# Embedding tiles, quarter tiles and early output chunks placed in TensorE's waits of a two-block transformer kernel

## The reference

```python
x = x + concat([rms(mla), rms(diff) * (1 - lam_init), rms(chunk)]) @ w_out[l]
x = x + conv_ffn(rms(x), ...)
# second block
x = layer_norm(ALPHA * x + h, ln1_g, ln1_b)
x = layer_norm(ALPHA * x + mlp(x) + sigmoid(x @ w_ple_gate + b) * (p[l] @ w_ple), ln2_g, ln2_b)
```

## Time and profile before

| what | value |
|---|---|
| median of 3 runs | 3014.87 us (3014.5 to 3016.16) |
| profiled execution | 3012.1 us, its span 3010.4 us |
| TensorE busy | 2929.3 us, 97% |
| VectorE, ScalarE, POOL busy | 1367.7, 840.3, 1363.9 us |
| mean granted clock of TensorE | 0.989 of full |
| chain that ended last | TensorE 93%, VectorE 3%, ScalarE 2% |

### The profile page before, as it was taken

The page is one execution under the profiler, slowest core; times in us unless marked ns, Lnnn a source line. Parts: engine busy times, 40 slices in busy tenths (PEclk is TensorE's granted clock), DMA queues, the critical chain, the costliest instruction groups (busy, mean ns, idle before and its releaser), DMA issues.

```text
span 3010.4 us, 40838 instructions
## 1 busy us (share of the span) xinstructions
PE 2929.3 (97%) x14072; PEld 2409.9 (80%) x14072; DVE 1367.7 (45%) x3149; ACT 840.3 (28%) x1874; POOL 1363.9 (45%) x924
## 2 busy tenths in 40 slices
PE   8999999999999999999999999999999999999998
PEld 6777788887777888878888778888788888788886
DVE  6484525244474525344773642112447745421124
ACT  3363212022363212121553230001325532300013
POOL 4322555564213555555233545555453336455553
PEclk9999999999999999999999999999999999999999
DMA  7322556564323555555333655556453336455563
GB/s 257 109 88 91 182 195 191 194 216 152 107 71 127 179 194 189 198 193 189 105 126 119 202 167 191 190 186 204 160 182 113 119 120 211 167 195 190 182 207 106
DMA packets 136521, 494.16 MB, mean 164 GB/s; under 512 B 15280, under 2 KB 15536, under 8 KB 136112
## 3 DMA queue, kind: packets, MB, share of 16 engines
q0 software_dynamic: 66240, 241.20, 25.0%
q1 hardware_dynamic: 68544, 245.40, 23.9%
q10 hardware_dynamic: 1584, 5.46, 0.5%
HBM read 489.91 MB, written 2.10 MB: 163 GB/s over the span
## 4 chain that ended last, share of the span: by engine, by line
PE 93%; DVE 3%; ACT 2%; issue 1%; DMA 0%; POOL 0%; SPq 0%; DVEq 0%; POOLq 0%; ACTq 0%
PE ps L554 26%; PE ps L555 25%; PE ps L556 25%; PE ps L732 3%; PE ps L755 2%; PE ps L801 2%; PE ps L681 2%; PE ps L682 2%; PE ps L683 2%; PE ps L745 1%; PE ps L793 1%; PE ps L782 1%; PE ps L783 1%; DVE tmp L1643 1%; DVE lo L1100 0%
## 5 line engine op out<-in xcount | busy, mean ns | idle before, releaser
L554 PE MATMUL ps<-hi,w_hi 128*128 128x512 f32 x3216 | 1274.0, 396 | 12.8 <-DVE lo L1100 6.8
L555 PE MATMUL ps<-hi,w_lo 128*128 128x512 f32 x3216 | 1257.8, 391 | 0.0
L556 PE MATMUL ps<-lo,w_hi 128*128 128x512 f32 x3216 | 1257.2, 391 | 0.0
L527 POOL TENSOR_TENSOR w_lo<-w_raw,w_hi 128x1024 fp32r<-128x1024 f32 x460 | 1106.3, 2405 | 90.6 <-DMA w_hi<-weights 80.3
L522 POOL DMA_DIRECT2D w_hi<-weights x460 | 261.1, 568 | 1520.0 <-PE ps L556 1390.1
L554 PEld LDWEIGHTS ps<-hi,w_hi 128*128 128x128 f32 x3216 | 606.3, 189 | 165.6 <-issue 31.8
L556 PEld LDWEIGHTS ps<-lo,w_hi 128*128 128x128 f32 x3216 | 606.2, 188 | 128.3
L555 PEld LDWEIGHTS ps<-hi,w_lo 128*128 128x128 f32 x3216 | 607.0, 189 | 118.7 <-issue 1.4
L1914 ACT ACTIVATE ps<-hb,col 128x512 f32<-128x512 f32 x88 | 68.6, 782 | 381.2 <-DVE hb L1129 381.2
L1670 DVE SCALAR_TENSOR_TENSOR x<-x,ps 128x512 f32<-128x512 f32 x64 | 43.9, 687 | 287.1 <-PE ps L556 287.1
L2040 ACT ACTIVATE sq<-ps 128x512 f32<-128x512 f32 x64 | 38.2, 597 | 464.2 <-PE ps L556 464.2
(11 more groups left out here) (342 smaller groups left out, 3242.3 us busy)
## 6 DMA issues: line engine op xcount, KB each, us to landing
w_raw<-weights SPq DMA_DIRECT2D x460, 512.0 KB, 3.3
w_hi<-weights POOLq DMA_DIRECT2D x460, 512.0 KB, 3.7
x<-xt SPq DMA_DIRECT2D x8, 256.0 KB, 10.0
out<-x SPq DMA_DIRECT2D x8, 256.0 KB, 2.0
kc<-k ACTq DMA_DIRECT2D x1, 1346.0 KB, 5.7
bias<-relb ACTq DMA_DIRECT2D x2, 512.0 KB, 5.0
bias<-relb ACTq DMA_DIRECT2D x1, 1024.0 KB, 4.9
praw<-pt ACTq DMA_DIRECT2D x2, 512.0 KB, 3.4
```

What stands on the lines that cost most here:

```text
L527: nc.gpsimd.tensor_tensor(wlo[s][:, :], raw[s][:, :], whi[s][:, :].bitcast(F32), ALU.subtract).then_inc(w_split, 1)
L554: nc.tensor.matmul(out_ap, w[0], xx[0], start=first, stop=False)
L555: nc.tensor.matmul(out_ap, w[1], xx[0], start=False, stop=False)
L556: return nc.tensor.matmul(out_ap, w[0], xx[1], start=False, stop=last)
```

## The change

In words, part by part:

- First attention: one quarter tile is done ahead of `all_read`, and iteration 0 has one instead of two. The tasks come in the order d 0-7, c 0-7, d 8-23, c 8-15, m 0-23. The factors of the d and c outputs are computed at iteration 44. Chunks 0 to 4 (three d, two c) are scaled at iterations 46, 48, ... 54, transposed two iterations later, their high halves made at +3 and the low halves at +4. At iterations 64 to 66 and just after it, chunks 0 to 4 of the first pair of `w_out` are multiplied; only the three m chunks are scaled, transposed and split after the last task. The rows of `w_out` are reordered to suit. The probabilities' buffers lie elsewhere in the freed input, and the bank ring after the attention starts with bank 2.
- Second attention: the two quarters of iteration 0 come ahead of `all_read`.
- Norms: `root_table` takes a root of one element early, so that the table is loaded before the row's root is wanted (the LayerNorms, the final norm and the end of the first attention). VectorE centers three chunks ahead of the spread's wait and chunks 5, 6, 7 later. One dummy matmul call instead of two.
- LayerNorm 1: embedding tile 0 goes ahead of the wait for the row's root, tiles 1 to 3 behind the spread in place of the dummies; ScalarE copies them out between its chunks. p is loaded and split before the output projection, and the weight unit moves in the stream.

```diff
@@ tasks_1
-            return d[0:8] + c_[0:8] + d[8:24] + m_ + c_[8:16]
+            return d[0:8] + c_[0:8] + d[8:24] + c_[8:16] + m_
@@ constants
-        S_BANK, TO_BANK, C_BANK = (4, 5, 6), (7, 0, 1), (4, 5, 6, 7)
+        S_BANK, TO_BANK, C_BANK = (4, 5, 6), (7, 0, 1), (2, 3, 2, 3, 2, 4, 5, 6)
-        QUARTERS.update({14: 4, 15: 0})
+        AHEAD_1 = 1
+        QUARTERS.update({0: 2 - AHEAD_1, 14: 4, 15: 0})
-        AT_FACTOR, AT_SCALE = 60, 62
+        AT_FACTOR, AT_SCALE, N_TURN = 44, 46, 5
+        SCALE_AT = [AT_SCALE + 2 * k for k in range(N_TURN)]
+        AT_PAIR = 64
@@ TensorE, first attention
+                    elif it - 2 in SCALE_AT:
+                        c = SCALE_AT.index(it - 2)
+                        turn_chunk(outs[c], c, oneed)
+                    elif it >= AT_PAIR:
+                        pair_chunk(it - AT_PAIR, A, oneed)
...
+                quarters(AHEAD_1, A)
                 all_read()
                 attention_1(TASKS["1", l], slots_1(l), fill)
-                for c, src in enumerate(dn + mn):
-                    turn_chunk(src, c)
...
-                dense(8, A, NC_, need, (4, turn_last))
+                for c in range(3, N_TURN):
+                    pair_chunk(c, A, oneed)
+                for c in range(N_TURN, NC_):
+                    turn_chunk(outs[c], c, oneed)
+                for c in range(N_TURN, NC_):
+                    pair_chunk(c, A, oneed)
+                dense(6, A, NC_)
@@ TensorE, norms
+            def embed(pneed, js):
+                for j in js:
+                    tile(q.unit % 4, BANK[q.tile], j * P, 4 * P, P, (phi, plo), (0, 1), pneed, q.unit + 1,
+                         USE[q.tile]).then_inc(w_used if j == 3 else part_done, 1)
+                    q.tile += 1
+                q.unit += 1 if 3 in js else 0
+            def factor_from_row(pneed=None):
+                if pneed is not None:
+                    embed(pneed, [0])
                 q.root += 1
                 pe.wait_ge(row_rooted, q.root)
...
-                keep_busy(2, kc2[:, K2["cos"]:K2["cos"] + S])
+                if pneed is not None:
+                    embed(pneed, [1, 2, 3])
+                else:
+                    keep_busy(1, kc2[:, K2["cos"]:K2["cos"] + S])
@@ TensorE, second attention
+                quarters(FILL[0], A)
                 all_read()
@@ VectorE
+                    if it - 4 in SCALE_AT:
+                        low_turned(SCALE_AT.index(it - 4))
...
-                for c in (2, 3):
+                for c in (2, 3, 4):
                     center(c)
...
-                    if i + 4 < NC_:
-                        center(i + 4)
+                    if i in (0, 3, 4):
+                        center({0: 5, 3: 6, 4: 7}[i])
@@ ScalarE
+            def root_table():
+                A_(spare, ident[0:1, 0:1], ACT.Sqrt)
...
+                    elif it == len(TASKS["1", l]):
+                        root_table()
+                    elif it - 3 in SCALE_AT:
+                        high_turned(SCALE_AT.index(it - 3))
...
+            def embedded(j):
+                tile_ready(last=(j % 4 == 3))
+                A_(pes[j][:, :], ps[:, BANK[q.tile], :], ACT.Copy).then_inc(free(), 1)
...
+                if which == 1:
+                    embedded(0)
                 for c in range(NC_):
...
+                    if which == 1 and c in (1, 2, 3):
+                        embedded(c)
```

More of the change, by code:

```diff
@@ L217, in build @@
             ck[b] = [c_(f"ck{b}_{i}", [P, S]) for i in range(2)]
-            c_ = carve(buf_at[b], buf_at[b] + 16 * KB2)
-            pr[b] = [c_(f"pr{b}_{i}", [P, S]) for i in range(6)]
-            pT[b] = [c_(f"pT{b}_{i}", [P, S]) for i in range(2)]
+            free_at = [buf_at[b] + k * KB2 for k in (13, 14, 15, 5, 11, 12, 6, 7)]
+            pr[b] = [place(f"pr{b}_{i}", [P, S], F32, free_at[i]) for i in range(6)]
+            pT[b] = [place(f"pT{b}_{i}", [P, S], F32, free_at[6 + i]) for i in range(2)]
         EARLY = 25
@@ L803, in attention, with pair_chunk @@
                         last.then_inc(pv_done, 1)
+            def pair_chunk(kc, src, need):
+                if kc == 0:
+                    pe.wait_ge(lo_ready, need + N_TURN)
+                    for j in range(2):
+                        pe.wait_ge(w_split, q.unit + j + 1)
+                        pe.wait_ge(d_free[BANK[q.tile + j]], USE[q.tile + j])
+                pe.wait_ge(lo_ready, need + kc + 1)
+                w = slice(kc * P, (kc + 1) * P)
+                for j in range(2):
+                    slot = (q.unit + j) % 4
+                    last = product(ps[:, BANK[q.tile + j], :], (whi[slot][:, w], wlo[slot][:, w]),
+                                   (src[0][:, kc, :], src[1][:, kc, :]), kc == 0, kc == NC_ - 1, None)
+                    if kc == NC_ - 1:
+                        last.then_inc(w_used, 1)
+                if kc == NC_ - 1:
+                    q.unit += 2
+                    q.tile += 2
             def keep_busy(n, rows):
@@ L846, in item @@
                         q.unit += 3
+                oneed = q.chunk
+                q.chunk += NC_
+                dn, mn, cn = natural_out(l)
+                outs = dn + cn + mn
                 def fill(it):
@@ L1004, in _ @@
                 dense(5, B, NC_)
-                layer_norm()
+                pneed = q.chunk
+                q.chunk += 2
+                layer_norm(pneed)
                 need = q.chunk
@@ L1016, in _ @@
                 for r in range(2):
-                    for j in range(4):
-                        tile(q.unit % 4, BANK[q.tile], j * P, 4 * P, P, (phi, plo), (0, 1), pneed, q.unit + 1,
-                             USE[q.tile]).then_inc(w_used if j == 3 else part_done, 1)
-                        q.tile += 1
-                    q.unit += 1
                     if r:
+                        embed(pneed, range(4))
                         dense(4, A, NC_)
@@ L1436, in _ @@
                 dve.wait_ge(fac_ready, 2 * l + 2)
-                for i in range(2):
-                    scale_rows(cn[i], fac[:, 28:32])
-                for c in range(1, 8):
+                for i in range(3):
+                    scale_rows(mn[i], fac[:, 28:32])
+                for c in range(N_TURN, NC_):
                     low_turned(c)
@@ L1645, in _ @@
                     low(o[:, :], B, c)
+                dve.wait_ge(aux_in, 32 + 16 * (L + 1) + 16 * l)
+                for c in range(2):
+                    low(praw[:, c, :], (phi, plo), c)
                 for c in range(NC_):
@@ L1654, in _ @@
                 layer_norm(l, 1, False)
+                q.tile += 4
+                q.unit += 1
+                q.part += 3
                 for g in range(FF2_GROUPS):
-                    if g == 1:
-                        dve.wait_ge(aux_in, 32 + 16 * (L + 1) + 16 * l)
-                        for c in range(2):
-                            low(praw[:, c, :], (phi, plo), c)
                     for c in range(8):
@@ L1672, in _ @@
                 for r in range(2):
-                    q.tile += 4
-                    q.unit += 1
-                    q.part += 3
+                    if r:
+                        q.tile += 4
+                        q.unit += 1
+                        q.part += 3
                     for j in range(4):
@@ L1838, in _, with high_turned @@
                 landed = lambda name: (d_free[BANK[tile_1(l, name)]], USE[tile_1(l, name)] + 1)
+                gains = ([pcol("diff_norm", l, i) for i in range(3)] + [pcol("ch_out", l, i) for i in range(2)]
+                         + [pcol("mla_out", l, i) for i in range(3)])
+                def high_turned(c):
+                    q.chunks += 1
+                    act.wait_ge(chunk_turned, q.chunks)
+                    A_(A[0][:, c, :], ps[:, C_BANK[c], :], ACT.Copy, scale=gains[c]).then_inc(hi_ready, 1)
                 def side(it):
@@ L2046, in _ @@
                 for r in range(2):
-                    for j in range(4):
-                        tile_ready(last=(j == 3))
-                        A_(pes[4 * r + j][:, :], ps[:, BANK[q.tile], :], ACT.Copy).then_inc(free(), 1)
+                    if r:
+                        for j in range(4):
+                            embedded(4 + j)
                     for j in range(4):
@@ L2134, in weight_stream @@
         full(a["w_out_2"][l])
+        unit(a["w_ple_2"][l][:, 0:512])
         for g in range(FF2_GROUPS):
```

104 lines of the change are left out of this document (49 added, 55 removed).

## The result

The changed kernel takes 2978.6 us (median of 4 runs, 2971.9 to 2991.3) against 3014.7 (3010.6 to 3016.2) for the one before on the same chip: ratio 0.9885, 95% interval 0.9858 to 0.9911. The forecast was 2982.5 with a range of 2972 to 2997. The profiled execution took 2977.4 us; its span of 2975.8 is 34.6 less than before, where the working gave 32.5.

The account below looks back on a forecast made before the run. TensorE, busy 97% of the span, was taken as the bound, so gains came only from its idle and lower-clock time. Terms of 2.8, 5.2, 2.4, 7.2, 11.5, 1.2 and 2.2 summed to 32.5 off 3014.87: 2982.5 us, 8-in-10 range 2972 to 2997.

Parts of the forecast that it names:

- LayerNorm 1: Embedding tiles fill the waits for root and spread at no price, and the root comes 0.25 earlier: 11.5 us for two.
- The clock after the gaps: Shorter gaps at the attention starts mostly spare layer 1's half-clock products: 2.4 us gained, bounds -3.4 and 3.6.
- First attention, end: Of 9.5 us lost there per layer, five expected losses keep 5.9: gain 3.6 a layer, 7.2 in all.
- (1): First attention's end: two table loads at iteration 44 with no filler beside them, a loss of 1.7 us per layer.
- (2): First attention's end: half clock after the stall at iteration 44, a loss of 1.0 us per layer, between 0 and 1.7.
- (3): First attention's end: ten more VectorE passes in 13 iterations, a loss of 1.2 us per layer, 1.8 at most.
- (4): After the last task: normalising, root, scaling and one chunk outlast the products and transposes, a loss of 1.0 us per layer.
- (5): First attention's end: five restarts of a product group between other work, 0.2 us each, a loss of 1.0 per layer.
- Rival A: The first attention's end gains nothing, as stall, half clock and VectorE's passes eat it: 2990 to 2995 us; chance 0.25.
- D: Slower: turned chunks at the first attention's end bind the engines in a circle, 3025 us at 5 a chunk; chance 0.04.
- rival C: Preloading the root's table fails and each norm loads twice more: 2993 us; chance 0.05.
- rival B: Half clock falls on moved work: embeddings -4.8, attention starts 0 instead of 2.4, final norm another 1: 2991 us; chance 0.11.

Follow-up runs that it names:

- starts_undone: The changed kernel with the quarter tiles back behind the wait on all banks in both attentions; 2992.7 us.
- held_5: The changed kernel with the embedding's weight unit released only after chunk 5 of the pair of tiles that follows LayerNorm 1; 2973.4 us.
- two_splits: The changed kernel with each GpSimd split of a weight unit made as two instructions of 512 columns instead of one of 1024; 2978.7 us.
- end_alone: Only the reordered end of the first attention, with the change's other parts put back as in the kernel before; 3000.4 us.
- norm_loads_undone: The changed kernel without the three early root_table calls of the norms, the one at iteration 64 kept; 2979.8 us.
- items_late: The changed kernel with latent items Q4, Q5 and K2 moved from iterations 32-34 to 45-47, K2 releasing the three weight units; 2974.4 us.
- items_released: As items_late, but the three weight units are released at iteration 56 by the first transpose of chunk 4, not by K2; 2967.5 us.
- both edits together: The changed kernel with the edits of held_5 and items_released; 2964.2 us.

## Why the prediction was right, step by step

The total was right (34.6 of span against 32.5 worked out), with two terms wrong in opposite directions: the attention's end gave 7.2 us more than its sum, LayerNorm 1 4.3 less. That they nearly cancel was luck, and so is the fit to 4 us of a median whose executions lie 19 us apart. Of its signs, the embedding tiles, the loads, the value evictions and the pace from iteration 40 came as written; "no wait on low halves follows in LayerNorm 1" did not.

- **First attention, start** (2.8). Right: in layer 0 the time from the block's first sums (L635, now L639) to the first scores is the same with one quarter more in it (33.0 and 32.9), and from there to the tail's start it is shorter by 1.4.
- **Second attention, start** (5.2). Right: 2.8 a layer in the start stretch at full clock.
- **The clock after the gaps** (2.4). Right for these places: in layer 1 the second attention's start gave 4.3, 1.5 of it clock, and the first attention is 2.6 shorter up to the tail, 1.2 of it clock. In the profiled execution a new half-clock stretch at 1555 took some 1.6 back, so the net was about 1 us. The bounds had that; by the earlier trace rows and starts_undone, whether such a gap costs at all is chance.
- **First attention, end** (3.6 a layer). Wrong in size: the tail is 7.2 shorter. Of the five losses expected, (1) was 1.6 against 1.7. (2), half clock after the stall, was 0 against 1.0 in every tail that had the stall; the 6.3 us of four tails came from half clock behind an earlier wait, of 0.85 for K, which the sum didn't have. (3), VectorE's extra passes, cost nothing: TensorE set the pace, at 6.36 for four tasks. (4) was a wait of 0.36 against 1.0. (5) was the restarts; the rows show 0.06 at a restart (0.29 for 0.23 at 255.14 and 257.42), not 0.2. So of 5.9 lost, some 2.3 stood. The 9.5 that went into the sum held the half clock of 10.2 us a layer; how much of the 7.2 is clock and how much the shorter chain, no run separates. Rival A, which had 0.25, was only true where the clock fell; D was nowhere near.
- **LayerNorm 1** (11.5 for two). Wrong: 3.4 and 3.7, together 7.2. The failing sentences are that TensorE "is never again ahead of a low half", and that the weight unit "is one of four prefetched ones, and POOL and SP idle through the norm". POOL did idle before; moving the embedding's unit into the norm puts a release there, and so a split, beside low halves. The pair started at +4.6, as worked out (+4.4), but ended at +18.1 behind the spread's end instead of +15.4; in held_5, without the collision, TensorE reaches the wait for w_lo at 1745.62, +15.8. The remaining wait for w_lo there is the other side of the same unit.
- **LayerNorm 2, end** (1.2). Too high, within its bounds: 1.1 less in layer 0 (85.95 to 84.82 from L978 to the next first scores), but 0.7 more at the end (20.6 to 21.4), where half clock stood for the last 14 us in place of the last 7. The root came 0.17 earlier, not 0.25.
- **Final norm** (2.2). Right: 2.1, of it 1.27 the load, with nothing for a drain, and so by difference 0.85 for the dummies.
- **Preloading** (rival C) worked: no load stands behind the sums.
- **Half clock on the moved work** (rival B) did not come at the embeddings; the final norm's products ran at 0.23. Behind LayerNorm 2 of layer 0 it did come (2145.5 to 2153), as it had before (2170.5 to 2178).

The Trainium skill (SBUF — State Buffer, Who interferes with whom) says that a VectorE instruction with two SBUF inputs contends with a GpSimd instruction that reads SBUF, and that one with at most one SBUF input, outside the two-port modes, doesn't. The trace agrees: 3.15 for lo<-tmp,kc,hi beside a split, while of the 88 records of L1501, which take one large operand from PSUM, the 82 that overlap a split take 0.75 us each, as the other 6 do:

```profile
L1501 DVE SCALAR_TENSOR_TENSOR ps<-hb,col,ps 128x512 f32<-128x512 f32 x88 | 65.9, 749 | 1.0 <-ACT ps L1971 1.0
```

Read against the prediction it would have named the collision: a low half of VectorE and a split of 2.41 us in the same norm.

## What to carry to other kernels

When work that frees a weight buffer is moved, the release moves with it, and with the release whatever GpSimd does on it. Look where that lands beside VectorE's operations with two inputs in SBUF, and place the release, not only the work. A factor that is read as a second tensor counts as an input there (the scaling vd<-vd,small, 3.15 us beside a split); the column of L1501, given as a scalar, didn't. A stall that frees a slot can be filled by work from elsewhere only if that work's release goes to a harmless place too. And where medians jump by more than the edit, compare stretches of equal work between two instructions; where the clock stays up, the tails and feed stretches here repeat within 0.1 us.

## What the runs showed of the hardware beyond that

- The collision lengthens work that no edit touched. In the gates stretch the additions of two SBUF tiles take 1763 ns on average in the changed kernel and the products with a PSUM operand 680. Groups of VectorE by shape (count, busy us, mean ns):

```profile
L1685 DVE TENSOR_TENSOR tmp<-tmp,tmp 128x512 f32<-128x512 f32 x16 | 28.2, 1763 | 2.0 <-DVE tmp L1681 0.5
...
L1681 DVE TENSOR_TENSOR tmp<-gate_o,ps 128x512 f32<-128x512 f32 x8 | 5.1, 680 | 0.0
```

  Of the 26 gates stretches in the table, 17 take 102.4 to 103.0 us, and in none of them does TensorE wait for these products (L1681); in the other nine, 104.3 to 109.3, it waits 1.6 to 5.6 us for them, and one (108.1) has 3.4 us of half clock besides. Both happen in the same code at the same place: 108.1 in the changed kernel, 102.6 in held_5, layer 0. The additions are long in both kinds (1794 and 1777 ns on average in these two), so it is where the collisions fall that differs; that the phase of POOL against VectorE sets this is argued, not shown. Timeline of the former:

```profile
1662.21 2.41 POOL L531 TENSOR_TENSOR w_lo<-w_raw,w_hi 128x1024 fp32r<-128x1024 f32 x1
1662.78 2.40 DVE L1098 TENSOR_TENSOR lo<-tmp,hi 128x512 fp32r<-128x512 f32 x1 [0.70 <-ACT hi L1745]
```

- It is a block, not a sharing. In the changed kernel's trace 45 operations of VectorE with two 128x512 SBUF operands start behind the start of a split that they meet. Each ends behind the split's end, 31 of them by 0.55 or 0.56 us, whether they met 2.3 us of it or 0.3, and the other 14 by 0.92 to 0.97. The splits hardly pay for it: those with VectorE beside them take 2.41 us on average, the others 2.40. Of the operations that start up to 0.6 us ahead of a split, 5 are blocked in the same way (3.12 to 3.31 us), and 15 keep their 0.69 to 0.74 while the split grows, to 2.89 in place of 2.41 at most. Which of the two it will be, the start alone doesn't tell.
- VectorE stays blocked through two GpSimd instructions that follow each other at once (two_splits, 3.27 us for 1.30 + 1.28).
- Half clock can begin 0.1 to 0.3 us behind a wait of only 0.85 and last 13.7 us (end_alone, norm_loads_undone, held_5; 4 tails), or not come at all behind the same wait (the changed kernel and 14 tails in all). In the six tails of items_late, items_released and both edits together, that wait is 0.52, and none had it; six are too few to say that the shorter wait is why. What decides it was not found.
